# Key rotation ahead of the first quad, and the bias additions on GpSimd instead of VectorE

## What is computed

```python
h = rms_norm(x, norm_mix)
qa, ka, va, qf, kf, vf, f_logit = split(h @ w_in)     # 16+4+4 and 16+16+16 heads of 64, 16 gates
out_a = swa_sink_attention(rope(qa), rope(ka), va, sinks)        # sliding window, GQA 16:4
log_f = log_sigmoid(f_logit + b_f)
out_b = forgetting_attention(qf, kf, vf, log_f)       # s + F[t] - F[s], F = cumsum(log_f), causal
x = x + concat(out_a, out_b) @ w_o
h = rms_norm(x, norm_ffn)
x = x + (silu(conv3(h @ w_up)[:, :5632]) * conv3(h @ w_up)[:, 5632:]) @ w_down
return rms_norm(x, norm_final)
```

## Time and profile before

| | |
|---|---|
| runs | 1084.99, 1087.52, 1086.70 us; median 1086.7 us |
| the profiled execution | 1084.99 us, of which the span from first to last instruction is 1083.2 us |
| busy in the span | PE 1072.1 us (99%), DVE 718.2 us (66%), ACT 587.3 us (54%), POOL 13.2 us (1%) |
| granted TensorE clock, mean | 0.998 of full speed |

### The profile page before, as it was taken

One profiled execution on the slowest core, in us unless ns is written; L12 is line 12 of the kernel. 1 busy time (PEld: TensorE's weight loads), 2 busy tenths in 40 slices (PEclk: granted clock), 3 DMA queues, 4 the chain that ended last, 5 costly groups with the idle time before them and its releaser, 6 DMA issues.

```text
span 1083.2 us, 17777 instructions
## 1 busy us (share of the span) xinstructions
PE 1072.1 (99%) x6137; PEld 924.3 (85%) x6137; DVE 718.2 (66%) x1044; ACT 587.3 (54%) x903; POOL 13.2 (1%) x34
## 2 busy tenths in 40 slices
PE   8999999999999999999999999999999999999997
PEld 8888889898888888888888888888888888888885
DVE  5687666676555777778777777778777444454543
ACT  6946475755555655555556555555555434343432
POOL 1200000000000000000000000000000000000000
PEclk9999999999999999999999999999999999999999
DMA  9775545454555666556665666656666655555552
GB/s 277 218 242 171 163 149 174 136 174 152 178 175 178 188 185 198 183 175 203 192 185 174 197 193 195 190 172 202 190 190 214 212 185 188 193 189 186 188 192 100
DMA packets 169794, 201.66 MB, mean 186 GB/s; under 512 B 8580, under 2 KB 136292, under 8 KB 169632
## 3 DMA queue, kind: packets, MB, share of 16 engines
q1 hardware_dynamic: 168464, 197.49, 58.3%
q0 software_dynamic: 976, 3.37, 0.9%
q10 hardware_dynamic: 320, 0.34, 0.1%
HBM read 199.06 MB, written 2.11 MB: 186 GB/s over the span
## 4 chain that ended last, share of the span: by engine, by line
PE 98%; DMA 1%; SPq 0%; DVE 0%; ACT 0%; issue 0%; DVEq 0%
PE tr_ps L1233 15%; PE pj L1233 15%; PE pj L994 9%; PE pj L1235 8%; PE tr_ps L1235 8%; PE sc_ps L982 5%; PE sc_ps L984 5%; PE sc_ps L983 5%; PE pj L996 5%; PE tr_ps L982 4%; PE tr_ps L984 4%; PE tr_ps L983 4%; PE pj L982 3%; PE pj L983 3%; PE pj L984 3%; DMA nat<-x 1%
## 5 line engine op out<-in xcount | busy, mean ns | idle before, releaser
L656 DVE TENSOR_TENSOR lo<-raw,hi 128x1024 fp32r<-128x1024 f32 (+1 forms) x368 | 446.1, 1224 | 273.6 <-ACT hi L408 273.3
L408 ACT ACTIVATE hi<-raw 128x1024 fp32r<-128x1024 f32 (+1 forms) x368 | 384.8, 1058 | 239.1 <-PE sc_ps L984 78.9
L1233 PE MATMUL tr_ps<-act_split,hi 128*128 128x512 f32 x704 | 245.3, 391 | 0.0
L1233 PE MATMUL pj<-act_split,hi 128*128 128x512 f32 x704 | 245.0, 391 | 0.0
L1235 PE MATMUL pj<-act_split,lo 128*128 128x256 f32 x704 | 197.1, 280 | 0.0
L1235 PE MATMUL tr_ps<-act_split,lo 128*128 128x256 f32 x704 | 197.1, 280 | 0.0
L1233 PEld LDWEIGHTS pj<-act_split,hi 128*128 128x128 f32 x704 | 131.6, 187 | 28.9
L1233 PEld LDWEIGHTS tr_ps<-act_split,hi 128*128 128x128 f32 x704 | 131.7, 187 | 28.8
L994 PE MATMUL pj<-act_split,hi 128*128 128x512 f32 x416 | 148.2, 400 | 0.0
L1235 PEld LDWEIGHTS tr_ps<-act_split,lo 128*128 128x128 f32 x704 | 133.0, 189 | 0.1
L1235 PEld LDWEIGHTS pj<-act_split,lo 128*128 128x128 f32 x704 | 133.1, 189 | 0.0
(11 more groups left out here) (197 smaller groups left out, 1224.7 us busy)
## 6 DMA issues: line engine op xcount, KB each, us to landing
raw<-w_up SPq DMA_DIRECT2D x176, 512.0 KB, 4.4
raw<-w_down SPq DMA_DIRECT2D x88, 512.0 KB, 4.5
raw<-w_in SPq DMA_DIRECT2D x72, 512.0 KB, 3.6
raw<-w_o SPq DMA_DIRECT2D x32, 512.0 KB, 3.8
nat<-x SPq DMA_DIRECT2D x8, 256.0 KB, 6.1
key_bias<-nft_dram POOLq DMA_DIRECT2D x4, 512.0 KB, 6.9
result<-nat SPq DMA_DIRECT2D x7, 256.0 KB, 3.1
gfin<-norm_final POOLq DMA_DIRECT2D x1, 1024.0 KB, 7.0
```

The costliest lines, as they stand in the source:

```text
L408: act.activation(hi[:, slot, 0:n], raw[:, slot, 0:n], ACT.Copy).then_inc(hi_done, 1)
L656: dve.tensor_tensor(lo[:, slot, 0:n], raw[:, slot, 0:n], hi[:, slot, 0:n].bitcast(F32), ALU.subtract).then_inc(lo_done, 1)
L1233: pe.matmul(up_banks[v][b].rearrange("p (a n) -> p a n", a=2), wh[:, c, b * P:(b + 1) * P], act_split[:, :, k, :], start=k == 0, stop=Fals ...
```

## The change

`rope_swap(1.0)` and the four copies to `kta` go from ACT's slots 0 and 2 of the first quad to the end of its part for tiles 4 to 7, ahead of the split of tile 11, with the wait for DVE's rotation between them. DVE's rotation goes from slot 1 to the same place, ahead of its split of tile 11, and writes a new buffer `rope_b`, which lies under the later `key_bias`. POOL's start waits for `kta_s` as well, `copy_group_a(0)` moves ahead of the DMAs, and POOL does the eight additions to `key_bias` in place of DVE.

```diff
-BIAS_SLOTS = [6, 9, 10, 11]
+        rope_b = sb("rope_b", [P, 2, S])
@@ gpsimd
+            pool.wait_ge(kta_s, 4)
             pool.wait_ge(evac_a, 1)
...
+            copy_group_a(0)
             pool.tensor_copy(fq[:], fcum[:, :, 0:4]).then_inc(fq_s, 1)
...
-            pool.wait_ge(kta_s, 4)
-            copy_group_a(0)
+            pool.wait_ge(d_tab, 64)
+            for n in range(4):
+                pool.wait_ge(d_bias[n], 16)
+                kb = key_bias[:, 4 * n:4 * n + 4, :]
+                mask = mask_b[:].unsqueeze(1).broadcast_to([P, 4, P])
+                pool.tensor_tensor(kb[:, :, 0:P], kb[:, :, P:2 * P], mask, ALU.add)
+                pool.tensor_tensor(kb[:, :, 2 * P:384], kb[:, :, 2 * P:384], mask, ALU.add).then_inc(bias_s, 1)
@@ scalar, for s == 3 of the tiles 4 to 7
                                    scale=-1.0).then_inc(fcum_s, 1)
+                    act.wait_ge(evac_d, 1)
+                    rope_swap(1.0)
+                    act.wait_ge(krope_s, 1)
+                    for h in range(2):
+                        for e in range(2):
+                            act.activation(kta[h * 64:h * 64 + 64, e::2, :], rope_b[e * 64:e * 64 + 64],
+                                           ACT.Copy).then_inc(kta_s, 1)
@@ scalar, quad
-                    elif s == 0:
-                        act.wait_ge(evac_d, 1)
-                        rope_swap(1.0)
-                    elif s == 2:
-                        act.wait_ge(krope_s, 1)
-                        for h in range(2):
-                            for e in range(2):
-                                act.activation(kta[h * 64:h * 64 + 64, e::2, :], qa[e * 64:e * 64 + 64], ACT.Copy).then_inc(kta_s, 1)
@@ vector, for s == 3 of the tiles 4 to 7
                     join_halves(1, rope_a, 1)
+                    dve.wait_ge(swap_s, 1)
+                    rope(rope_b, 1.0).then_inc(krope_s, 1)
@@ vector, quad
-                    if s == 1 and not attend:
-                        dve.wait_ge(swap_s, 1)
-                        rope(qa, 1.0).then_inc(krope_s, 1)
                     if s == 7:
-                        if not attend:
-                            dve.wait_ge(kta_s, 4)
                         dve.wait_ge(swap_s, j + 2)
...
-                    elif s in BIAS_SLOTS:
-                        dve.wait_ge(d_bias[n], 16)
-                        dve.tensor_tensor(kb[:, :, 0:P], kb[:, :, P:2 * P], mask, ALU.add)
-                        dve.tensor_tensor(kb[:, :, 2 * P:384], kb[:, :, 2 * P:384], mask, ALU.add).then_inc(bias_s, 1)
```

More of the change, by code:

```diff
@@ L528, in quad @@
                         attention(s + NEXT, j - 1)
-                    elif s == 0:
-                        act.wait_ge(evac_d, 1)
-                        rope_swap(1.0)
-                    elif s == 2:
-                        act.wait_ge(krope_s, 1)
-                        for h in range(2):
-                            for e in range(2):
-                                act.activation(kta[h * 64:h * 64 + 64, e::2, :], qa[e * 64:e * 64 + 64],
-                                               ACT.Copy).then_inc(kta_s, 1)
                     elif s == 1:
@@ L801, in quad @@
                         dve.memset(never, -1e30).then_inc(never_s, 1)
-                    elif s in BIAS_SLOTS:
-                        n = BIAS_SLOTS.index(s)
-                        dve.wait_ge(d_bias[n], 16)
-                        kb = key_bias[:, 4 * n:4 * n + 4, :]
-                        mask = mask_b[:].unsqueeze(1).broadcast_to([P, 4, P])
-                        dve.tensor_tensor(kb[:, :, 0:P], kb[:, :, P:2 * P], mask, ALU.add)
-                        dve.tensor_tensor(kb[:, :, 2 * P:384], kb[:, :, 2 * P:384], mask, ALU.add).then_inc(bias_s, 1)
                     attention(s, j)
```

## The result

The changed kernel takes 1093.68 us (median of 4 runs, 1092.77 to 1094.76) against 1085.99 us; the ratio is 1.0069, with a 95% interval from 1.0052 to 1.0088: 0.69% slower, some 7.5 us. The forecast was 1089.1 us and its range ended at 1092.8.

A forecast was written before the change was run, and what follows sets the result against it. PE was taken as the bound, waiting for nobody where the change acts. A 2.4 us stall at tile 11, all else hidden, on the runs' median of 1086.7 us gave 1089.1 us, range 1087.2 to 1092.8.

The forecast's parts named there:

- What bounds the kernel: Whole kernel: PE, busy 1072.1 of 1083.2 us, waits for nobody where changed; any new wait is paid in full.
- The key rotation, moved: Ahead of tile 11's split: the serial ACT-DVE-ACT-DVE chain makes PE start tile 11 2.4 us late, bounds 2.15 to 2.6.
- What is late next: Tiles after 11: later splits and loads stay in time, the lead is rebuilt, no second stall out of this part.
- POOL's order: POOL's queue: bias loads start 5 us later, at 53.4, and land between 59 and 65.5; costed at nothing.
- The eight additions: POOL, from 59 to about 70 us: eight additions at 1.1 us each, 9 us, by themselves hidden.
- Where POOL and DVE meet: SBUF access: POOL stood still under a two-input DVE operation, 0.98 against 0.19 us; if mutual, additions hold up DVE.
- rival 1: Tile 19: additions take turns with DVE, a second stall of 2.7 us, total 5.1, 1091.8 us; chance 0.33.
- Rival 2, the clock,: Stall at tile 11: granted clock falls to half, one tile costs 2.8 us more, 1091.9 us; chance 0.04.
- The sum of the cases: Whole time: stall alone 0.45, rivals priced singly; range 1087.2 to 1092.8 us takes in rival 1 at full price.

The follow-up runs named there:

- experiment 7: Changed kernel with the key rotation moved behind tile 11's split and the eight additions given back to DVE; 1088.12 us, ratio 1.0030.
- experiment 9: Changed kernel with rotation behind tile 11's split, additions on DVE, and bias loads issued only once tile 14 is split; 1085.73 us, ratio 0.9996.
- experiment 1: Changed kernel with the eight bias additions given back to DVE, the rotation still ahead of tile 11; 1089.07 us, ratio 1.0033.
- experiments 2 and 3: Changed kernel with POOL's additions held until tile 19's split is done, 1090.53 us; kernel before with only the additions moved to POOL, 1087.47 us.
- experiment 3: Kernel before with only the eight bias additions moved to POOL, behind its three small copies; 1087.47 us, ratio 1.0017.
- experiment 5: Changed kernel with tile 11's split put ahead of the swap copies and the rotation, additions still on POOL; 1094.10 us, ratio 1.0078.

## Why the prediction was wrong

- **What bounds the kernel** held in the main. PE waited for nobody in that stretch, no run was faster than before beyond its interval, and every wait made there was paid at once; up to 0.9 us of it came back over the rest of the span (0.4 in the changed kernel).
- **The key rotation, moved.** Right in mechanism and size: a wait at tile 11 alone, forecast at 2.4 us start to start, measured 2.2 (2.20 to 2.22 in the five profiles that have it). The hand-over to PE that no row showed was 50.32 less the end of the split at 50.26, 0.06 us, where I took 0.25: the one term of this sum that was mis-sized.
- **What is late next** missed something that the first stall hid. I said "no second stall out of this part". Once tile 11 is split first, the late `nft` puts the bias loads ahead of tile 18's load, which costs about 2 us (2.1 us at PE's end in experiment 7, none in experiment 9). With the stall in place, tile 18's load went out 0.24 us ahead of the bias loads, and PE was late anyway.
- **POOL's order.** The bias loads started at 54.31 less the later start of 0.65, 53.7, forecast 53.4. Their landing was forecast until 65.5; it was 68.5, 67.9 with the same 0.65 off. I costed this at nothing, and it cost no wait by itself, but it thinned the margin: in experiment 1 the load of tile 19, the first one behind them, landed at 69.7, and the split was over 1.9 us before PE started the tile, where I had reckoned 3.2.
- **The eight additions.** 1.28 us each, forecast 1.1.
- **Where POOL and DVE meet** is the first step that failed. I had the row (0.98 against 0.19 us) and the mechanism, and gave the case a third; the exclusion is mutual, and the two engines take turns operation by operation. It is rival 1 that happened: the second wait at tile 19, forecast 2.7 us, measured 2.3 start to start. DVE's operations from the split of tile 18 to that of tile 19 were stretched by 5.7 us in sum, where rival 1 had 5.8.
- **Rival 2, the clock,** is the second. I gave it 0.04 on the ground of a window in which the clock had not fallen while PE stood idle. That window lies too near the last matmul to tell. In the same profile the clock fell at 1079.8, 4.1 us behind the last matmul; with waits of about 2 us the clock fell at the restart or up to 1.5 us behind it, not in the wait itself. It fell behind the wait at tile 11 in four profiles and not in experiment 1's. Each fall behind a wait of about 2 us cost 1.5 to 1.7 us.
- **The sum of the cases.** I priced the rivals one at a time, so that the range ended where one of them would be. They were not alternatives: 2.2 + 1.7 + 2.3 + 1.7 are 7.9 of the 8.2 us at tile 24. Here a stall of about 2 us brought a fall of the clock with it in six cases of seven.

What stays open: the small difference of 0.3 us between tiles 12 and 18 in the changed kernel (seen in three other profiles too, absent in experiments 2 and 3), why tile 18's load landed 1.2 us later in experiment 3, and what decides whether the clock falls behind a wait of 2.06 us.

## What to carry to other kernels

Where TensorE never waits, count for each prepared tile how early it is, and cost a moved chain by the tile behind it; moving a serial ACT-DVE-ACT chain ahead of a split turned free gaps into 2.2 us. Work given from VectorE to GpSimd came back where GpSimd read SBUF under VectorE's two-input operations: put it at a time when that work has slack, and count each operation on either side as nearly the sum of both (1.78 us for 0.69 and 1.28). When two costs sit in one stretch, undoing one alone may show nothing (1.0078 against 1.0069): the later deadline swallows part of the earlier delay, and PE's longer wait there can cost a longer fall of the clock. A bulk transfer's cost lies in which urgent load it goes ahead of, not in its own lateness.

## What the runs showed of the hardware

- The granted clock fell to half around the restart after six of seven PE waits of 1.9 to 2.1 us (from 0.1 us ahead of it to 1.5 us behind), at a cost of 1.5 to 1.7 us each, and not after waits of 0.52 to 1.34 us. In the wait of 4.46 us of experiment 5 it fell 0.9 us before the restart and cost 2.8 us. Filling the waits with matmuls kept it full.
- GpSimd and VectorE: an addition of 128x512 took 1.28 us alone, 1.74 with a rotation step in front of it and up to 2.3 with a split in front of it; a VectorE step with two SBUF inputs 0.69 alone, 1.09 beside one-input copies, 1.78 beside two-input additions, 0.69 beside memsets.
- A 512 KB weight load took 3.5 us in quiet and 9.4 to 12.8 us as the first one issued behind the start of four bias loads of 512 KB each from the other queue; issued 0.2 to 0.4 us ahead of them it took 5.0 to 10.8 us.
